# Neighbourhood attention: turned probabilities copied ahead of the next mask, queries scaled on ScalarE, block sums of the weights on VectorE

## The reference, cut to what matters

```
qkv = (h @ w_qkv).reshape(B, S, 3, N_HEADS, HEAD_DIM)
q = qkv[:, :, 0] * (HEAD_DIM ** -0.5)
...
s = jnp.einsum('brqhd,brikhd->bhrqik', qg[:, :, q0:q0 + NA_QCOLS], kb)
s = jnp.where(valid[:, None, :], s + bias, -jnp.inf)
p = jax.nn.softmax(s.reshape(B, H, rows, NA_QCOLS, kr * NA_KCOLS), axis=-1)
outs.append(jnp.einsum('bhrqik,brikhd->brqhd', p, vb))
```

## Time and profile before

| what | value |
|---|---|
| median of three runs | 4283.18 us (4280.76 to 4284.72) |
| profiled execution | 4280.6 us, of which the span is 4278.5 us |
| busy share of the span | TensorE 91%, VectorE 50%, ScalarE 23%, GpSimd 20% |
| neighbourhood stage | about 1662 to 2203 us of the span |
| TensorE busy from 1706 to 2146 us | 416.0 of 440 us, granted clock 0.99 |
| VectorE busy in the same stretch | 282.9 of 440 us |

### The profile page before, as it was taken

The page is one execution under the profiler, slowest core; times in us unless marked ns, Lnnn a source line. Parts: engine busy times, 40 slices in busy tenths (PEclk is TensorE's granted clock), DMA queues, the critical chain, the costliest instruction groups (busy, mean ns, idle before and its releaser), DMA issues. The chain is left out here.

```text
span 4278.5 us, 78593 instructions
## 1 busy us (share of the span) xinstructions
PE 3890.7 (91%) x33982; PEld 2391.4 (56%) x33982; DVE 2156.9 (50%) x3195; ACT 997.6 (23%) x1736; POOL 854.2 (20%) x654
## 2 busy tenths in 40 slices
PE   8999998899999998999989999875999999999973
PEld 4555654445555545665545567553666664566642
DVE  4555356446554556666666322215566787522214
ACT  3333223133332221222210000003444440000002
POOL 2222011032211100111100433320221300233320
PEclk9999999999999999999999999997999999999996
DMA  4233102332321213444442899983000111699995
GB/s 139 94 108 100 60 20 89 87 109 99 99 94 30 94 40 90 74 78 84 73 166 104 348 419 379 422 366 112 16 1 16 40 37 74 262 419 392 407 421 243
DMA packets 237283, 674.58 MB, mean 158 GB/s; under 512 B 60195, under 2 KB 163363, under 8 KB 209159
## 3 DMA queue, kind: packets, MB, share of 16 engines
q1 hardware_dynamic: 216519, 627.42, 41.0%
q0 software_dynamic: 16896, 33.63, 2.1%
q10 hardware_dynamic: 3520, 8.44, 0.5%
HBM read 621.40 MB, written 52.02 MB: 157 GB/s over the span
## 5 line engine op out<-in xcount | busy, mean ns | idle before, releaser
L2926 DVE TENSOR_TENSOR sb_work<-sb_work,ps 128x256 f32<-128x256 f32 (+2 forms) x66 | 33.7, 510 | 669.7 <-ACT sb_work L2913 669.7
L490 PE MATMUL ps<-sb_mixT,sb_work 128*128 128x512 f32 x768 | 358.8, 605 | 8.6 <-ACT sb_x_tok L836 5.5
L490 PE MATMUL ps<-sb_xT,sb_work 128*128 128x512 f32 x768 | 356.9, 602 | 8.6 <-ACT sb_x_tok L836 5.5
L2913 ACT ACTIVATE sb_work<-ps 128x256 f32<-128x256 f32 (+2 forms) x66 | 30.1, 456 | 994.5 <-PE ps L2881 994.5
L490 PEld LDWEIGHTS ps<-sb_mixT,sb_work 128*128 128x128 f32 x768 | 138.4, 192 | 148.5 <-issue 131.7
L490 PEld LDWEIGHTS ps<-sb_xT,sb_work 128*128 128x128 f32 x768 | 137.7, 191 | 147.6 <-issue 130.8
L2881 PE MATMUL ps<-sb_work,sb_xT 128*32 128x256 f32 x3136 | 186.7, 401 | 32.3 <-DMA sb_work<-moe_w_up 28.8
L2896 PE MATMUL ps<-sb_work 128*32 128x256 f32 x3776 | 212.7, 379 | 0.0
L2812 POOL DMA_INDIRECT scratch_y<-sb_work,sb_const x176 | 176.5, 1003 | 163.5 <-DVE sb_work L2939 113.4
L2881 PE MATMUL ps<-sb_work,sb_mixT 128*32 128x256 f32 x3136 | 179.0, 389 | 27.1 <-DMA sb_work<-moe_w_up 23.7
L2312 DVE TENSOR_REDUCE sb_cols<-ps 128x1 f32<-128x1024 f32 x128 | 150.7, 1219 | 84.8 <-PE ps L2123 84.7
(11 more groups left out here) (528 smaller groups left out, 7436.9 us busy)
## 6 DMA issues: line engine op xcount, KB each, us to landing
sb_work<-moe_w_down SPq DMA_DIRECT2D x42, 2048.0 KB, 21.0
sb_work<-moe_w_gate SPq DMA_DIRECT2D x30, 2048.0 KB, 8.6
sb_work<-moe_w_up SPq DMA_DIRECT2D x30, 2048.0 KB, 13.4
sb_xT<-moe_w_gate SPq DMA_DIRECT2D x15, 2048.0 KB, 14.8
sb_xT<-moe_w_up SPq DMA_DIRECT2D x15, 2048.0 KB, 20.3
sb_mixT<-moe_w_gate SPq DMA_DIRECT2D x15, 2048.0 KB, 15.2
sb_mixT<-moe_w_up SPq DMA_DIRECT2D x15, 2048.0 KB, 21.0
sb_work<-w_in SPq DMA_DIRECT2D x56, 512.0 KB, 4.4
```

The lines of the kernel that those rows point to most:

```text
L490: last = pe.matmul(m.ps[:, bank, :], b.w[i][:, k, :], m.xT[:, k, half * HALF:(half + 1) * HALF], start=(k == 0), stop=(k == NK - 1))
L2913: act.activation(b.act[n % 2][:, 0:strips[n], :], strip_sums(2 + 2 * (n % 2))[:, 0:strips[n], 0:P], ACT.Silu).then_inc(silued, 1)
L2926: dve.tensor_tensor(act, act, strip_sums(2 + 2 * (n % 2))[:, 0:strips[n], P:2 * P], ALU.mult).then_inc(multiplied, 1)
```

## The change

VectorE copies the turned probabilities (`copy_out`) before the next half's mask, not after it; the pieces of the first batch move with the copy, those of the second batch stay behind the mask. GpSimd does nothing in the stage any more. The queries are scaled after the projection, by ScalarE: the low half in the copy that evicts piece P2, the high half in place in one instruction at t=1, for which the scores of t=4 wait. The block sums of the weights are made by VectorE at t=1, for the next pair, from unscaled weights.

```diff
@@ -1689,7 +1689,7 @@
                     elif j == P1:
-                        pe.wait_ge(w_scaled, pair + 1)
+                        pe.wait_ge(loaded[2], 16 * (pair + 1))
                     elif j == P6:
                         pe.wait_ge(w_sums_ready, pair + 1)
@@ -1723,7 +1723,7 @@
                 elif t == HALF_TILES:
-                    pe.wait_ge(added, len(DVE_READS) * (pair + 1))
+                    pe.wait_ge(q_scaled, pair + 1)
@@ -1803,8 +1803,12 @@
                 else:
-                    act.copy(q[pair % 2][:, 0:HALF].rearrange(...), src.rearrange(...)).then_inc(evicted, 1)
+                    act.mul(q[pair % 2][:, 0:HALF].rearrange(...), src.rearrange(...), -HD ** -0.5).then_inc(evicted, 1)
+
+            def scale_high(pair):
+                act.wait_ge(added, len(DVE_READS) * (pair + 1))
+                act.mul(q[pair % 2][:, HALF:], q[pair % 2][:, HALF:], -HD ** -0.5).then_inc(q_scaled, 1)
@@ -1819,6 +1823,8 @@
                 done = done_by(pair, t)
+                if t == 1:
+                    scale_high(pair)
                 if i + 1 < count:
                     exp(i + 1)
@@ -1832,22 +1838,17 @@
-        @block.gpsimd
-        def _(pool):
-            ...
-                pool.tensor_scalar(w[2], w[2], -HD ** -0.5, None, ALU.mult).then_inc(w_scaled, 1)
-            ...
         @block.vector
         def _(dve):
             masks = Steps(dve, masked)
+
+            def sum_weights(pair):
+                for j in range(1, 3):
+                    dve.wait_ge(loaded[j], 16 * (pair + 1))
+                dve.tensor_tensor(T3, B22, B12, ALU.subtract)
+                masks.settle(dve.tensor_tensor(T1, B12, B11, ALU.subtract))
+                masks.settle(dve.tensor_tensor(T2, B22, T1, ALU.subtract))
+                dve.tensor_tensor(T4, B21, T2, ALU.subtract).then_inc(w_sums_ready, 1)
@@ -1928,6 +1929,7 @@
             dve.tensor_tensor(S4, A12, S2, ALU.subtract).then_inc(x_sums_ready, 1)
+            sum_weights(0)
             wait_bias(0)
@@ -1942,16 +1944,18 @@
                     normalise(i + 1)
+                if pair + 1 < pairs:
+                    for piece in range(done[0], done[1]):
+                        add(PIECES + piece)
+                copy_out(i)
                 if u + 1 < 2 * pairs and b in (1, 2):
                     wait_bias(u + 1)
                     mask(u + 1, b - 1)
                 if pair + 1 < pairs:
-                    for piece in range(done[0], done[1]):
-                        add(PIECES + piece)
-                copy_out(i)
-                if pair + 1 < pairs:
                     for piece in range(done[1], done[2]):
                         add(PIECES + piece)
+                    if t == 1:
+                        sum_weights(pair + 1)
                 finish(i)
```

More of the change, by code:

```diff
@@ L1588, in neighbourhood_stage @@
      weighed, finished) = (s[f"signal_{n}"] for n in range(1, 14))
-    added, x_sums_ready, w_scaled, w_sums_ready, x_back = (s[f"signal_{n}"] for n in range(14, 19))
+    added, x_sums_ready, q_scaled, w_sums_ready, x_back = (s[f"signal_{n}"] for n in range(14, 19))
     pairs, count = D // P, NA_STEPS
@@ L1805, in evict @@
                 else:
-                    act.copy(q[pair % 2][:, 0:HALF].rearrange("p (b r c) -> p r b c", b=HALF_TILES, c=NA_COLS),
-                             src.rearrange("p (r b c) -> p r b c", b=HALF_TILES, c=NA_COLS)).then_inc(evicted, 1)
+                    act.mul(q[pair % 2][:, 0:HALF].rearrange("p (b r c) -> p r b c", b=HALF_TILES, c=NA_COLS),
+                            src.rearrange("p (r b c) -> p r b c", b=HALF_TILES, c=NA_COLS), -HD ** -0.5).then_inc(evicted, 1)
+            def scale_high(pair):
+                act.wait_ge(added, len(DVE_READS) * (pair + 1))
+                act.mul(q[pair % 2][:, HALF:], q[pair % 2][:, HALF:], -HD ** -0.5).then_inc(q_scaled, 1)
             def exp(i):
```

## The result

| | before | after |
|---|---|---|
| median, us | 4282.34 (4 runs) | 4259.22 (4 runs, 4252.19 to 4261.5) |
| ratio | | 0.9943, 95% interval 0.9927 to 0.9959 |
| profiled execution, us | 4280.6 | 4261.5 |
| neighbourhood stage, first projection matmul to the first matmul of the next stage, us | 1666.11 to 2202.87: 536.8 | 1668.99 to 2183.11: 514.1 |

4260.6 was forecast, in a range of 4249 to 4273. This profiled execution came 2.9 us later to the stage than that of before, so its own time moved by less than the stage did: 19.1 us.

The account below looks back on a forecast made before the run. TensorE was taken as the pace in seven of eight pairs, idle 22.8 us before weighing because VectorE's copy was late. 13.3 + 5.0 - 1.3 + 5.6 = 22.6 us saved, median 4260.6, range 4249 to 4273.

Parts of the forecast that it names:

- The gap of t=1: TensorE's wait before weighing the values at t=1 goes in seven pairs: 13.3 us saved.
- Low clock behind it: Spells of low TensorE clock after the t=1 gap go: three seen, 1.7 us each, 5.0 us saved.
- the three terms of these pairs: Seven pairs: t=1 gap 13.3 us and low clock 5.0 us saved, 1.3 us lost at t=5 and t=6.
- The lag on VectorE at t=2: VectorE starts t=2 2 us late, yet its copy keeps 1.1 us slack: no gap before the weighing.
- The rival by which VectorE paces t=2: Block sums at 1.271 us each use up the slack, leaving 1.2 us a pair: 8.4 us, 4269; chance 8%.
- Block sums: Four 128x512 subtractions on VectorE at t=1, 0.69 us each, 2.8 us a pair, absorbed by the step.
- Scaling: ScalarE's extra 128x512 instruction a pair, before the exponentials of t=2; 0.3 to 4.8 us costs nothing.
- The price at t=5 and t=6: Two gaps, 1.36 us, become one of about 1.5 before the next pair's first scores: 1.3 us lost over seven pairs.
- the rival without a new gap: Additions of t=6 come in time, so no gap before the next scores: 10.5 us more saved, 4250; chance 9%.
- The last pair: At t=1 and t=2 of the last pair, 9.09 us between bias additions becomes 6.3: 5.6 us saved.
- The clock rival: The new 1.5 us gap brings low clock in each of seven pairs: 11.8 us cost, 4272; chance 17%.
- Late weights: VectorE stands at the t=1 block sums until weights land; some 15 us later gives 4289; chance 4%.

Follow-up runs that it names:

- the runs with longer gaps: Changed kernel plus one unread VectorE subtraction behind the mask of t=6, before the fourth piece's addition: 128x512, 4276.73 us; 128x1024, 4272.91 us.
- the run with 2.3: Changed kernel plus one unread VectorE subtraction of 128x512 behind the mask of t=6, before the fourth piece's addition: 4276.73 us, 0.9989.

## Why the prediction was right

- **The gap of t=1** was to go, and went, in all seven pairs. Its cause was told only in part: the prediction took VectorE's order to be late and GpSimd to make it later. It took both. The new order closes the gap with masks still up to 2.371 us, and the engine moves close it in the old order, where VectorE without GpSimd beside it is in time. The forecast did not hang on this, since the change removes both.
- **Low clock behind it**, 5.0 us forecast. None is left in the seven pairs. First to last end of a pair shrank from 438.9 to 421.5 us, by 17.4, where the three terms of these pairs were 13.3 + 5.0 - 1.3 = 17.0. That the stage then lost just the 22.6 of the sum is chance: 17.4 in the pairs and 5.9 from the end of the last piece to the end of the stage make 23.3, and 0.7 was lost at the start, where the low clock lasted 6.2 us from the first projection matmul, and 4.7 before. Chance too is a median within 1.4 us, with four runs 9 us apart.
- **The lag on VectorE at t=2** was to be absorbed with 1.1 us to spare. It was; the room measured 1.2. The rival by which VectorE paces t=2 became true only when the sums were made twice.
- **Block sums** taken at 0.69 us took 0.69. **Scaling** of the high half took 0.634 in idle time, and six more of it cost nothing.
- **The price at t=5 and t=6**: two gaps of 1.36 were to turn into one of 1.5, a loss of 0.2. It is 1.60, a loss of 0.24 in idle time; in the prediction's chain, the signal from VectorE to TensorE took 0.15 instead of 0.1. What holds the scores is shown from both sides: it grows with an instruction put ahead of L1872 and goes with the mask moved away. So the rival without a new gap is out.
- **The last pair**, 5.6 us forecast: 9.09 twice became 5.92 and 6.29, 6.0 us. The weighing of the first ran at the higher clock, and VectorE with the mask ended last there, as the prediction allowed.
- **The clock rival** had 17% and did not come: no spell behind a gap of 1.60 in the seven pairs of this kernel, nor in 28 more gaps of 1.60 and 1.70 in the runs with the order alone, the six scalings and the doubled sums, whose pairs from the second on are equal to 0.01 us. Its price was right, 1.5 to 1.7 us for a single spell in the runs with longer gaps, where 8 of 14 gaps of 2.3 and 2.9 were followed by low clock.
- **Late weights**: VectorE stood before the sums for nothing; the first sum follows the mask by 0.03 us.

Not settled: which part of a spread of 9 us among the changed kernel's four runs comes from where. Their spans differ while the pairs of every run that was profiled with this gap are equal to 0.01 us, so it hardly comes from these. That is not shown, as only one of the four was profiled.

## What to carry to other kernels

On an engine that serves a busier one in order, sort each step's work by who waits for it: what releases the busy engine now goes first, what is needed half a round later goes last, and what is moved behind must be checked for a reader that now stands behind it (here a piece's addition, 1.6 us a pair). When two edits attack the same wait, try each alone: here the wait of t=1 needed the old order and a slowed VectorE together, so either edit closed it, and the second bought nothing more there. Idle share says little about room: VectorE was idle for a third of the time and had 1.2 us to give at t=1.

## What the runs showed of the hardware that was not expected

In the first seven pairs, gaps of TensorE of 1.60 and 1.70 us were followed by no low clock in 35 cases, nor were the two of 1.57 and 1.58 before; the gap of 1.94 was followed by a spell, and so were two of the three of 2.5 to 2.6 before, 5 of 7 of 2.3 and 3 of 7 of 2.9. So the length of the gap alone does not decide, and the same kernel can lose 0 or 3.1 us at the same place: in the run with 2.3 the pairs after the first lay between 60.76 and 63.87 us. What does decide stays open.

GpSimd's subtractions slowed VectorE's normalisation too, which has one large input: 0.42 us without GpSimd, up to 1.40 beside it.
